# Two instructions moved up in the mixing stage: GpSimd's copy of the transformed half, VectorE's maximum of the logits

## What is computed

```python
h = rmsnorm(x, norm1_g) * (1 + mod[:, 1]) + mod[:, 0]
a, states = mixer(h, w_in, b_in, head_g, w_out, init, grid_w)
x = x + mod[:, 2] * a
h = rmsnorm(x, norm2_g) * (1 + mod[:, 4]) + mod[:, 3]
x = x + mod[:, 5] * expert_choice_moe(h, router_w, w1, w3, w2)
...
# end of mixer: hm is the mLSTM heads' output, fu the Fourier half
hm = hm * lax.rsqrt(jnp.mean(hm * hm, axis=-1, keepdims=True) + EPS) * head_g[:, None, :]
hm = hm.transpose(0, 2, 1, 3).reshape(B, T, MLSTM_WIDTH) * jax.nn.sigmoid(o)
out = jnp.concatenate([hm, fu], axis=-1).astype(h.dtype) @ w_out
...
# start of expert_choice_moe: the affinities of the tokens to 16 experts
aff = jax.nn.softmax((xf @ router_w).astype(jnp.float32), axis=-1)
gate, idx = lax.top_k(aff.T, cap)
```

## Time and profile before

| | us |
|---|---|
| median of 3 runs | 2321.66 (2321.58 to 2322.97) |
| the profiled execution, its time | 2321.6 |
| the profiled execution, its span | 2319.7 |
| TensorE busy | 2177.2 |
| VectorE busy | 489.0 |
| ScalarE busy | 351.3 |
| GpSimd busy | 271.2 |

### The profile page before, as it was taken

One profiled execution on the slowest core, in us unless ns is written; L12 is line 12 of the kernel. 1 busy time (PEld: TensorE's weight loads), 2 busy tenths in 40 slices (PEclk: granted clock), 3 DMA queues, 4 the chain that ended last, 5 costly groups with the idle time before them and its releaser, 6 DMA issues. The chain is left out here.

```text
span 2319.7 us, 37027 instructions
## 1 busy us (share of the span) xinstructions
PE 2177.2 (94%) x15031; PEld 1876.7 (81%) x15031; DVE 489.0 (21%) x1255; ACT 351.3 (15%) x995; POOL 271.2 (12%) x266
## 2 busy tenths in 40 slices
PE   7999999999982799999999999999999999999992
PEld 2444444875541799999999999999999999999992
DVE  1111115557657110111110011111011111001102
ACT  1111112133320110111111101111011111111102
POOL 0000000211120102202112021020220210202102
PEclk9999999999995899999999999999999999999996
DMA  9720101643317559789697797986978969769765
GB/s 376 304 100 32 63 32 46 236 161 123 127 55 228 173 177 363 217 298 297 233 365 216 252 351 221 337 251 242 363 217 290 305 231 366 216 246 358 220 246 182
DMA packets 351601, 528.69 MB, mean 228 GB/s; under 512 B 12996, under 2 KB 292284, under 8 KB 348232
## 3 DMA queue, kind: packets, MB, share of 16 engines
q1 hardware_dynamic: 336456, 509.28, 63.4%
q0 software_dynamic: 15104, 18.88, 3.9%
HBM read 492.17 MB, written 35.95 MB: 228 GB/s over the span
## 5 line engine op out<-in xcount | busy, mean ns | idle before, releaser
L1675 PE MATMUL ps_ab<-xeT,ring 128*128 128x144 f32 x8192 | 1008.6, 286 | 14.6 <-DVE xeT L1720 14.6
L1675 PEld LDWEIGHTS ps_ab<-xeT,ring 128*128 128x128 f32 x8192 | 1006.9, 190 | 14.7 <-issue 14.7
L1688 PE MATMUL ps_yy<-hidT,ring 128*128 128x144 f32 x4096 | 504.4, 286 | 0.0
L1688 PEld LDWEIGHTS ps_yy<-hidT,ring 128*128 128x128 f32 x4096 | 502.8, 190 | 0.0
L465 PE MATMUL ps_p<-w_in_sb,hT 128*128 128x512 f32 x720 | 319.6, 597 | 2.1 <-ACT hT L333 2.1
L1724 DVE TENSOR_TENSOR hidT<-silu,ps_ab 128x144 f32<-128x144 f32 x256 | 78.0, 305 | 886.3 <-ACT silu L1642 827.0
L465 PEld LDWEIGHTS ps_p<-w_in_sb,hT 128*128 128x128 f32 x720 | 134.9, 191 | 157.7 <-issue 154.0
L1621 POOL DMA_INDIRECT stream<-ye,slot_row x64 | 101.0, 1578 | 1215.7 <-DVE ye_p L1735 1201.1
L1642 ACT ACTIVATE silu<-ps_ab 128x144 f32<-128x144 f32 x256 | 74.5, 291 | 909.2 <-PE ps_ab L1675 865.0
L1160 PE MATMUL b_z<-y,shared 128*128 128x512 f32 x288 | 129.6, 604 | 15.2 <-issue 6.5
L1160 PEld LDWEIGHTS b_z<-y,shared 128*128 128x128 f32 x288 | 53.8, 192 | 80.6 <-issue 77.6
(11 more groups left out here) (262 smaller groups left out, 1046.9 us busy)
## 6 DMA issues: line engine op xcount, KB each, us to landing
ring<-in_exp_w SPq DMA_DIRECT2D x384, 1024.0 KB, 12.3
y<-in_ada_w SPq DMA_DIRECT2D x22, 1024.0 KB, 7.9
w_in_sb<-in_w_in SPq DMA_DIRECT2D x4, 2048.0 KB, 21.4
shared<-kvo SPq DMA_DIRECT2D x15, 512.0 KB, 5.6
kvo<-pr SPq DMA_DIRECT2D x9, 768.0 KB, 3.3
qkT_dram<-qkT SPq DMA_DIRECT2D x9, 512.0 KB, 4.6
qk<-qkT_dram SPq DMA_DIRECT2D x9, 512.0 KB, 4.9
m_in<-m_lanes SPq DMA_DIRECT2D x9, 512.0 KB, 5.5
```

What stands on the lines that cost most here:

```text
L1675: mm = nc.tensor.matmul(ps_ab[f % 2][:, N * w:N * w + N], unit[:, k, bass.ts(c, P)], xeT[:, k], start=(k == 0), stop=(k == DT - 1))
L1688: mm = nc.tensor.matmul(ps_yy[d % 2][:, 0:N], unit[:, f % 2, bass.ts(d, P)], hT[:, f], start=(f == 0), stop=(f == FT - 1))
```

## The change

GpSimd's copy of the Fourier half goes from behind the three steps on the sums of squares to ahead of them, directly behind the power. Its waits and its semaphore stay. VectorE's maximum of the logits becomes a function `largest`, called in `outputs` between `hms_ready` and the gate's product where the turn has both a tile for `outputs` and one for the router (turns 4 to 9); in turns 10 to 12, without `outputs`, it stays where it was.

```diff
@@ gpsimd, turn
                         nc.gpsimd.tensor_tensor(hms[:], hms[:], g.minus_half[:], ALU.pow).then_inc(rh_ready, 1)
+                    if on(i, 1):
+                        if below(i, 2):
+                            pool.wait_ge(f_kept, PAIRS // 2 + 1)
+                            pool.wait_ge(kv_summed, TILES - 1)
+                        elif not below(i, 3):
+                            pool.wait_ge(out_summed, 2 * i - 4)
+                        nc.gpsimd.tensor_copy(mixT[:, 1 - par, HEADS:DT], g.fuT[:, :, bass.ts(i - 1, P)]).then_inc(mix_pool, 1)
                     if on(i, 2):
...
-                    if on(i, 1):
-                        if below(i, 2):
-                            pool.wait_ge(f_kept, PAIRS // 2 + 1)
-                            pool.wait_ge(kv_summed, TILES - 1)
-                        elif not below(i, 3):
-                            pool.wait_ge(out_summed, 2 * i - 4)
-                        nc.gpsimd.tensor_copy(mixT[:, 1 - par, HEADS:DT], g.fuT[:, :, bass.ts(i - 1, P)]).then_inc(mix_pool, 1)
@@ vector
+                def largest(i):
+
+                    dve.wait_ge(logits_turned, i - 3)
+                    did(nc.vector.tensor_reduce(soft[:, 0:1], b_z[1][:, 0:E], AX.X, ALU.max, negate=True), negmax_ready)
+
@@ outputs
                     did(TS(hms[:], hms[:], 1.0 / HD, EPS, ALU.mult, ALU.add), hms_ready)
+                    if on(i, 4):
+                        largest(i)
                     dve.wait_ge(o_loaded[1 - par], 16 * (half + par))
@@ turn
                         outputs(i, par, half)
-                    if on(i, 4):
-                        dve.wait_ge(logits_turned, i - 3)
-                        did(nc.vector.tensor_reduce(soft[:, 0:1], b_z[1][:, 0:E], AX.X, ALU.max, negate=True), negmax_ready)
+                    elif on(i, 4):
+                        largest(i)
```

## The result

The changed kernel takes 2304.03 us (median of 4 executions, 2303.77 to 2306.05) against 2321.62 us of before: a ratio of 0.9925, 95% interval 0.9912 to 0.9937. It is 17.6 us faster. The profiled execution took 2304.07 us, its span is 2302.2.

The account below looks back on a forecast made before the run. TensorE was taken to bound the kernel, also in the mixing stage. 13.1 (copy) + 1.7 (clock) + 2.7 (maximum) = 17.5 us; 2321.6 - 17.5 = 2304.1, with 0.2 for the port 2304.3 us; range 2302.5 to 2309.

Parts of the forecast that it names:

- the four "issue" ones: Before L1160's first half: four of eight waits listed as "issue", read from clock times as waits for GpSimd's copy.
- Part 1: Moving GpSimd's copy ahead of the sum of squares removes eight waits before the projection's first half, turns 3 to 10: 13.1 us.
- The clock in turn 3: Without the 2.05 us gap, turn 3's projection avoids the lower TensorE clock, 7.13 us instead of 8.80: 1.7 us gained.
- Part 2: Moving VectorE's maximum ahead of the gate's product starts the projection's second half earlier in turns 4 to 8: 2.7 us.
- Part 3: VectorE work queued behind the maximum, and the copy's port conflicts, stay mostly hidden: 0 to 0.2 us late.
- the cover: Slack of VectorE's second weighting before TensorE's L1276 needs it: 0.4 us plus 0.1 in turn 5; just enough in turn 3.
- The signs named: No first-half waits, turn 3's L1160 about 7.1 us, maximum 0.3 us after L1256's start, second half 1.0 after, turns 21.8.
- The clock did not fall: Rival: TensorE's clock falls all the same, in turn 3 or once elsewhere; 1.7 us less gained, 2306.0 us; chance 0.12.
- The order does act: Answers the rival that the projection's first half waits for something else at the same moment: 2321.7 us, chance 0.02.
- VectorE is not the bound: Answers the rival that ports make VectorE bound the middle turns: 2315.9 us, halfway 2307 to 2311; chance together 0.11.
- The slower case: Rival: VectorE's second weighting comes so late that L1276 waits past its old place: 2328.5 us, chance 0.03.

Follow-up runs that it names:

- the two experiments on turn 2's copy: Kernel before with only turn 2's copy moved ahead of the sums of squares: 2317.93 us; changed kernel with only that copy in its old place: 2307.72 us.
- the maximum alone: Changed kernel with GpSimd's copy put back behind the three steps on the sums of squares, VectorE's maximum still moved: 2319.39 us, ratio 0.9989 to before.
- turn 2's copy back: Changed kernel with only turn 2's copy put back behind the sums of squares: 2307.72 us.
- the copy alone: Changed kernel with VectorE's maximum put back behind `outputs`, GpSimd's copy still moved: median 2318.77 us; three later traced executions 2319.76, 2320.26 and 2324.88.
- four products: Changed kernel with four unused VectorE products added in `outputs` behind L1411, 2.9 us in each turn: 2323.09 us.
- the second set of executions: Changed kernel measured again without an edit: median 2305.31 us of 5 executions, ratio 0.9928 to the kernel before.

## Why the prediction was right

**What bounds, and which rows are the copy.** Right. All eight waits in front of the first half are gone, the four "issue" ones as well, so reading them as the copy from the clock times held.

**Part 1, 13.1 us.** Measured from start to start, the eight first halves gained 2.22 in turn 3, then 1.25, 1.38, 1.48, 1.38, 1.47, 1.73 and 1.72: 12.6 us. The mis-sized term is the matmuls of the router, taken as 1.76 us by the spacing of others; without a wait behind them they take 1.85, which is 0.1 us in each of seven turns.

**The clock in turn 3, 1.7 us.** Right in the traces: 1.77, shown by the two experiments on turn 2's copy. What I had not seen is that a fall doesn't follow each time. This gap of 2.05 us had one in each of the three traces that hold it (before, the maximum alone, turn 2's copy back), gaps of like size elsewhere had one in 5 of 20 (the copy alone) and in none of 6 (four products).

**Part 2, 2.7 us.** 0.56, 0.48, 0.47, 0.48 and 0.46 in turns 4 to 8, 2.5 us with the 0.03 of turn 9. The second half starts 1.01 to 1.02 us behind the turning in turns 4, 6 and 8, as worked out, but 1.09 in turns 5 and 7; why is open. That the copy alone would only move the wait to the second half is shown.

**Part 3, the cover.** The forecast of 0 to 0.2 us late was on the safe side. Counted from the start of L1208, the second weighting ended 19.45 us later before and 19.20 now (572.71 - 553.51): earlier by 0.25. The copy holds L1411 by 0.3, but the power takes 1.01 instead of 1.38, since the gate's product no longer runs ahead of it. The cover before L1276 is 0.87 us in turn 5, not 0.4 to 0.5: 0.25 from VectorE, and 0.2 because TensorE itself gained less there than forecast. In turn 3 it is 0.16, as thin as forecast, and it held.

The Trainium skill's rule (SBUF — State Buffer, Who interferes with whom) that the second to issue waits for the first agrees with the traces at three places: L1385 takes 1.62 us behind L981, L1411 0.98 instead of 0.69 behind the copy, and the power 1.38 instead of 1.01 behind the gate's product. At a fourth place they do not show it. In turn 5 of the changed kernel the gate's product starts at 565.92, while the power runs (565.49 to 566.50), and takes 0.68 us as ever; so it does in all six turns 4 to 9. The power is held when it comes second and holds nothing when it comes first, so the wait at the maximum, which lets the power start first, brings the pair to an earlier end.

**The sum.** 12.6 + 1.8 + 2.5 = 16.9 us in the stage, against 17.5. The whole came out at 17.5 in the span because 0.7 us was won by chance in the first 56 us; the second set of executions, with 2305.3 us, lies 1 us over the forecast of 2304.3. So that the number hit to 0.3 us is partly luck; that the sign, the size and each of the three terms came out is not. The signs named are there too: the maximum starts 0.3 us after L1256 (565.83 against 565.52), turns take 21.96 and 21.90 us rather than 21.8, and routing to the end took as long as before.

**Rivals.** The clock did not fall in turns 3 to 10. The order does act. VectorE is not the bound, but becomes it when its chain ends later by more than its cover, 0.87 us in turn 5 and 0.16 in turn 3. The slower case has its mechanism shown: with 2.9 us added L1276 waits 2 us in each turn and the kernel takes 2323.1 us. But 3.0 us of that lie ahead of turn 3, and the stage, 202.58 us, is still shorter than before.

No version here beats the changed kernel by more than can be told: the copy ahead of the power has the same time. What TensorE still waits for in the stage, 5.9 us on L1075 in turns 9 to 12, is another place.

## What to carry to other kernels

Where an engine that bounds the stage waits for two releasers in a row, closing the first gap alone can simply move it to the second, as it did here in turns 4 to 9: work out both positions, and change both together. An operation whose data is long ready should not stand in a queue behind a wait that it doesn't need, and what is put at the head of a queue with a wait of its own cost nothing here because the work behind it had a cover, so work that cover out first. Price a gap in front of matmuls not only by its length but by the slower clock that may follow it, and trace more than one execution before calling that price fixed.

## What the runs showed of the hardware that was not expected

- The granted TensorE clock after a gap differs between executions of one kernel at some lengths. In the kernel with the copy alone, 5 of 20 gaps of 1.99 to 2.30 us were followed by the lower level of 1.2 GHz for part of a projection, 1.7 us each, and the same gap had it in one execution and not in the next. None of the four gaps of 1.70 us had it. A single trace can't tell which.
- The length of the gap does not decide it alone. The gap of 2.61 us in turn 3 of the kernel with four products was followed by a clock of 1.00, those of 1.69 us in turns 11 and 12 of the changed kernel, where TensorE has little work, by router products of 3.29 and 3.57 us instead of 1.92. What decides is not shown.
- GpSimd's power on 128x4 elements takes 1.01 us when it starts ahead of VectorE's product or with none beside it, 1.38 when 0.17 us behind it, and 1.56 in the one turn where the two start within 0.01 us. VectorE's product takes 0.68 to 0.69 us in all these cases, also when it starts while the power runs. So in this pair only GpSimd's side is held; that the order of issue decides is read from these rows, not tested apart.
